# Taking 36 unread constant products out of the norms of a two-block model's second half

## The reference, cut to what matters

```python
for i in range(DEPTH_2):            # 4 layers: gdn, hgrn, gla, gdn
    m = mixer_i(x)
    x = layer_norm(DN_ALPHA * x + m, mix_ln_g[i], mix_ln_b[i])
    x = layer_norm(DN_ALPHA * x + swiglu(x, ffn_w_in[i], ffn_w_down[i]), ffn_ln_g[i], ffn_ln_b[i])
```

## Time and profile before

| | |
|---|---|
| median of 3 runs | 2442.35 us (2440.2 to 2442.55) |
| profiled execution | 2440.08 us, span 2438.4 us |
| PE busy | 2379.8 us, 98% of the span, 19026 products |
| DVE, ACT busy | 1754.9 us (72%), 1179.3 us (48%) |
| mean granted TensorE clock | 0.992 |

### The profile page before, as it was taken

The page is one execution under the profiler, slowest core; times in us unless marked ns, Lnnn a source line. Parts: engine busy times, 40 slices in busy tenths (PEclk is TensorE's granted clock), DMA queues, the critical chain, the costliest instruction groups (busy, mean ns, idle before and its releaser), DMA issues.

```text
span 2438.4 us, 49464 instructions
## 1 busy us (share of the span) xinstructions
PE 2379.8 (98%) x19026; PEld 2200.1 (90%) x19026; DVE 1754.9 (72%) x2902; ACT 1179.3 (48%) x1828; POOL 77.1 (3%) x149
## 2 busy tenths in 40 slices
PE   8999999999999999999999999999989999999998
PEld 6877877778998999988999998999989999988998
DVE  5788799988857876776666867665567657677665
ACT  5454522223655444566444555444555446566444
POOL 1000000000000000000400000000000000000000
PEclk9999999999999999999999999999999999999999
DMA  8433355555434555422555532555425554313553
GB/s 318 156 113 121 106 192 185 189 175 168 172 105 142 195 180 177 133 74 96 190 185 188 170 105 79 191 184 191 151 90 161 189 175 155 120 62 113 199 180 130
DMA packets 119715, 378.31 MB, mean 155 GB/s; under 512 B 11655, under 2 KB 29063, under 8 KB 119184
## 3 DMA queue, kind: packets, MB, share of 16 engines
q1 hardware_dynamic: 107040, 328.62, 40.9%
q0 software_dynamic: 12528, 47.62, 5.9%
HBM read 375.15 MB, written 1.05 MB: 154 GB/s over the span
## 4 chain that ended last, share of the span: by engine, by line
PE 78%; DVE 11%; issue 6%; ACT 3%; DMA 1%; DVEq 1%; SPq 0%; ACTq 0%
PE gb L610 20%; PE gb L611 20%; PE gb L612 20%; DVE w_lo L579 2%; PE mb L719 1%; DVE W L1629 1%; PE mb L612 1%; PE mb L611 1%; PE mb L610 1%; ACT w_hi L571 1%; DMA X<-in_x 1%; PE gb L3007 1%; DVE W L1253 1%; DVE W L1254 1%; PE gb L691 1%
## 5 line engine op out<-in xcount | busy, mean ns | idle before, releaser
L610 PE MATMUL gb<-Xs,w_hi 128*128 128x256 f32 (+1 forms) x3422 | 1035.8, 303 | 10.2 <-DVE w_lo L579 5.0
L612 PE MATMUL gb<-Xs,w_lo 128*128 128x256 f32 (+1 forms) x3422 | 1022.3, 299 | 0.0
L611 PE MATMUL gb<-Xs,w_hi 128*128 128x256 f32 (+1 forms) x3336 | 992.2, 297 | 0.0
L571 ACT ACTIVATE w_hi<-raw 128x1024 fp32r<-128x1024 f32 x582 | 610.4, 1057 | 679.9 <-PE gb L612 640.7
L579 DVE TENSOR_TENSOR w_lo<-raw,w_hi 128x1024 fp32r<-128x1024 f32 x582 | 705.4, 1222 | 210.0 <-ACT w_hi L571 199.7
L610 PEld LDWEIGHTS gb<-Xs,w_hi 128*128 128x128 f32 x3422 | 645.4, 189 | 57.7 <-issue 17.4
L612 PEld LDWEIGHTS gb<-Xs,w_lo 128*128 128x128 f32 x3422 | 645.2, 189 | 26.1
L611 PEld LDWEIGHTS gb<-Xs,w_hi 128*128 128x128 f32 x3336 | 629.2, 189 | 23.4 <-issue 1.9
L611 PE MATMUL gb<-Fs,w_hi 128*128 128x256 f32 (+1 forms) x966 | 277.7, 288 | 0.0
L610 PE MATMUL gb<-Fs,w_hi 128*128 128x256 f32 (+1 forms) x880 | 248.2, 282 | 0.7 <-ACT Pj L1778 0.7
L612 PE MATMUL gb<-Fs,w_lo 128*128 128x256 f32 (+1 forms) x880 | 247.2, 281 | 0.0
(11 more groups left out here) (472 smaller groups left out, 3230.9 us busy)
## 6 DMA issues: line engine op xcount, KB each, us to landing
raw<-in_up SPq DMA_DIRECT2D x264, 512.0 KB, 3.5
raw<-in_down SPq DMA_DIRECT2D x96, 512.0 KB, 3.7
R<-in_mod_later POOLq DMA_DIRECT2D x80, 512.0 KB, 3.8
raw<-in_gdn_in SPq DMA_DIRECT2D x64, 512.0 KB, 3.5
raw<-in_down SPq DMA_DIRECT2D x48, 384.0 KB, 4.0
raw<-in_hgrn_in SPq DMA_DIRECT2D x32, 512.0 KB, 4.4
raw<-in_ev_in SPq DMA_DIRECT2D x24, 512.0 KB, 4.2
raw<-in_gla_in SPq DMA_DIRECT2D x24, 512.0 KB, 4.0
```

Of the source, the lines that this page charges most:

```text
L571: nc.scalar.activation(hi, raw[:, slot, 0:hi.shape[1]] if len(hi.shape) == 3 else like(raw[:, slot], hi), ACT.Identity).then_inc(*hi_ready ...
L610: nc.tensor.matmul(to, weight_block(w_slot, 0, k), x_hi, start=start, stop=False)
L611: nc.tensor.matmul(to, weight_block(w_slot, 0, k), x_lo, start=False, stop=False)
L612: return nc.tensor.matmul(to, weight_block(w_slot, 1, k), x_hi, start=False, stop=stop)
```

## The change

`pe_warm` and its calls are taken out, in all eight places. Nothing is put in. PE stands still from the end of `pe_stats` until the first `h_ready`.

```diff
-        def pe_warm(pe, n):
-
-            for _ in range(n):
-                nc.tensor.matmul(mb[:, 0, :], ones[:, :], vec[:, 0:512], start=True, stop=True)
-
-        def pe_out(pe, n, ready, layer_norm=False, warm=5, order=tuple(range(KC)), rows=rows_of, aside={}):
+        def pe_out(pe, n, ready, layer_norm=False, order=tuple(range(KC)), rows=rows_of, aside={}):
...
             pe_stats(pe, n, layer_norm)
-            pe_warm(pe, warm)
...
-        def pe_ffn(pe, n, stats, layer_norm=False, warm=5, aside={}):
+        def pe_ffn(pe, n, stats, layer_norm=False, aside={}):
...
                 pe_stats(pe, stats, layer_norm)
-                pe_warm(pe, warm)
...
-            pe_out(pe, T, ready, warm=4, rows=mixed_rows, aside=OUT_ASIDE)
+            pe_out(pe, T, ready, rows=mixed_rows, aside=OUT_ASIDE)
...
-                    pe_ffn(pe, T, T, layer_norm=True, warm=4 if i < 3 else 0, aside=DOWN_ASIDE)
+                    pe_ffn(pe, T, T, layer_norm=True, aside=DOWN_ASIDE)
```

## The result

The changed kernel takes 2450.86 us (median of 5 runs, 2448.96 to 2454.06) against 2441.88 us before (5 runs, 2440.2 to 2442.55). The ratio is 1.0038, with a 95% interval of 1.0027 to 1.0049: 9.0 us slower, 6.6 to 12.0. Forecast were 2450.2 us and a range of 2444 to 2455. The profiled execution took 2450.67 us, its span is 2449.0 us, and the mean granted clock is 0.986. In its five executions that clock was 0.986 to 0.988. In all 59 executions of the kernel before that ran beside the experiments it was 0.990 to 0.995.

What follows compares the result with a forecast made beforehand. PE, busy 98%, was taken as the bound, though the removed products run beside the norm. Eight falls at 1.2 us less 1.8 us freed, +7.8 on 2442.35, gave 2450.2 us; range 2444 to 2455 us.

Steps and rivals of the forecast that it cites:

- The overrun: Constant products outlasting the norm: removal frees 0.32 us after each of four mixers, 0.5 after od, 1.8 us in all.
- A fall in each of the eight places: Granted clock falls to 0.50 around each new PE pause, 3.6 us in seven places and 2.7 us after od.
- The witness chosen: Kernel end, same sums without constant products after them: clock is 0.50 from 2431.7, 2.7 us after PE stopped.
- The rival of seven falls: Only the seven long pauses fall, od's 2.7 us does not: +6.6, 2449.0 us, chance 0.10.
- What one fall costs: Slow work after PE resumes, mean 2.6 us, costs 1.2 us of time a fall, bounds 0.5 and 1.6.
- the clock would be back after one stretch: Behind the pauses PE is dense, so each slow stretch was taken as a single one of some 3.4 us.
- a rival with 0.06: Slow stretches last twice as long: +20.6, 2463.0 us; in a third of the places +12, 2454; chance 0.06.
- The price of slow work: In the groups behind the pauses, 16 products against 30 in 3.2 us: each slow us costs 0.47 us.
- a fall isn't hidden: PE needs 0.96 us for nine products against DVE's 0.97 us a block: no slack, so the delay reaches the group's end.
- an assumed spread of starts: Slow stretches start evenly from 2.3 us ahead of PE's resumption to 1 us behind it.
- Sum: Over the eight places, 8 x 1.2 - 1.8 = +7.8 us, slower by 0.3%.
- The freed PE time: 72 removed passes at 0.43 us in each place, 31 us of PE time, mostly beside the norm and no gain.

Runs made afterwards that it cites:

- Experiment 1: Against the kernel before, constant products taken out after the first three FFNs of the second block alone; 2445.72 us against 2441.36, ratio 1.0018.
- number 3: Against the kernel before, four constant products in place of five after four mixers, three in place of four after od; 2438.02 us, ratio 0.9985.
- second profile: The changed kernel run once more without an edit; one execution, 2448.38 us.
- experiments 2, 3 and 6: Against the kernel before: od and four mixers without constant products, 2446.72 us; number 3; three products in each of eight places, 2440.75 us.

## Why the prediction was right

**The overrun** was forecast at 1.8 us and is 1.4: 0.21 to 0.28 in place of 0.32 us after each of four mixers, 0.37 in place of 0.5 after od, where the second block, which waits for its own `h_ready`, takes back part. The FFN places free nothing, as forecast.

**A fall in each of the eight places**: eight in both profiles. Experiment 1 shows that it isn't certain, with one place of three spared; over the four profiles that have pauses of 3.56 us, 20 of 21 fell. Eight of eight was likely, but not assured. The witness chosen was the right one, the end of the kernel, where the same sums are followed by nothing. Od fell at 2.7 us in all three profiles without its products, the seven places with one product and 2.69 us of pause fell five times, and the seven with 1.85 us once. The rival of seven falls is refuted by od. The Trainium skill ("TensorE: Matmul & The Clock Gate", section "Why this matters for your kernels") warns of idle gaps over about 3 us. These falls lie below it, so here the trace is stricter.

**What one fall costs** is the term that was mis-sized. It was put at 1.2 us. Over both profiles it is (14.0 + 12.3) / 16 = 1.6 us. The ten stretches of 3.4 us cost 1.25 us on the mean, close to the forecast's figure. The other six lasted 6.8 us and cost 2.3 us. The step that failed is the sentence that the clock would be back after one stretch because PE is dense behind our pauses. That holds if the stretch opens once PE works again or in the last half us of its wait. If it opens with 0.6 us or more of the pause left, it lasts twice as long. The forecast had this as a rival with 0.06, and its second figure, double stretches in a third of the places and 2454 us, was nearest to what the places did.

The price of slow work was misread as well. The 16 and 30 products in 3.2 us are those that overlap the window, not those that start in it. Two starts that follow each other at 0.50 (kernel before) and two at 1.00 (number 3):

```profile
1036.18 0.41 PE L612 MATMUL gb<-Xs,w_lo 128*128 128x256 f32 x1
1036.39 0.41 PE L610 MATMUL gb<-Xs,w_hi 128*128 128x256 f32 x1
```

```profile
1154.16 0.28 PE L612 MATMUL gb<-Xs,w_lo 128*128 128x256 f32 x1
1154.28 0.28 PE L610 MATMUL gb<-Xs,w_hi 128*128 128x256 f32 x1
```

Over longer stretches the distances are 0.213 and 0.117 us. So a us of slow work costs 1 - 0.117/0.213 = 0.45 us, not 0.47. And nine products need 9 x 0.117 = 1.05 us at full clock, not 0.96: PE is slower than the norm's 0.97 us a block and, but for some 0.2 us ahead of the second block, paces the group itself. That a fall isn't hidden was right all the same. The forecast's mean of 1.2 us for a single stretch came out close by an assumed spread of starts, not by a measured one.

**Sum.** By the first profile the places alone make 14.0 - 1.4 = +12.6 us, by the second 12.3 - 1.4 = +10.9, and the spans grew by 10.6 and 2446.7 - 2438.4 = 8.3 us. So 2.0 and 2.6 us came back elsewhere, which is why 7.8 us forecast and 9.0 measured lie so close. It is a balance of more than that. From the ACT split behind the first gdn layer's FFN to line 714 at the end of the hgrn mixer it is 161.57 us before and 155.98 after (155.74 in the second profile), so 5.6 us came back there. 1.5 us were added between od and the first gdn norm, 1.7 in the last FFN, and 0.4 in the rest. Windows in the first of these stretches, before and after (they differ in length, so only the clock is to be compared):

```profile
1345.00:1513.70 168.70, 161.20 (x1927) 155.40 (x1926) 125.06 (x171) 92.12 (x136) 0.00 (x0) 0.96 0.38 123
```

```profile
1360.00:1515.10 155.10, 148.69 (x1861) 143.44 (x1860) 119.23 (x156) 86.18 (x125) 0.00 (x0) 1.00 0.39 130
```

The slow stretches beside the thin products of line 3035 are absent in the profile after. The kernels of experiments 2, 3 and 6 (three products) show 0.98 and 0.99 there. Single executions of the kernel before differ by up to 10 us on one chip (2436.67 to 2446.96 us), and over these 27 the time goes with the mean granted clock: some 1.7 us less for each 0.001 more, with a correlation of -0.76. The changed kernel's clock is lower by 0.004 to 0.006, which at that rate, as an estimate, would be 7 to 10 us. Whether the change moved the falls between the places or they come and go from run to run was not tried and stays open. The forecast is right in its sign, its mechanism and its total, but the total owes something to errors that cancel: the places cost 3 to 5 us more than forecast, and 2.0 to 2.6 us came back elsewhere.

**The freed PE time** (31 us) bought nothing, as forecast: none of it had been in the way but the 1.4 us.

## What to carry to other kernels

Work that nobody reads may be holding the clock: before it is taken out, look in the trace for a place where the same sequence ends in a pause without it (the end of the kernel will do) and read the granted clock there. Then cost a fall at the slow work behind the pause, 0.45 us for each us here, and allow for a second stretch if the clock can fall before TensorE resumes. The gain was in trimming the filler to the length of the wait: one product fewer in five places made this kernel 1.5 to 5.9 us faster, of which 1.4 us is traced to these places; taking all of them out made it 9 us slower.

## What the runs showed of the hardware that was not expected

- A busy TensorE can lose its clock: with thin products of 16 columns and a busy share of 1.00 it fell in five of eight places.
- Slow stretches came in 3.4 and 6.8 us (10.2 us after od with thin products), and without constant products a stretch that opened 0.6 us or more before TensorE resumed was a long one in the norms of the second block, one that opened later a short one, in all profiles read here.
- The chance of a fall drops with the work placed in the pause: 8, 5, 1 and 0 of eight places for none (in two profiles), one, two and three products of 512 columns (in one profile each). By the length of the pause, outside od, it was 20 of 21 at 3.56 us, 5 of 7 at 2.69, 1 of 7 at 1.85 and none of 7 at 0.99.
